# Which queue issues the transfers that turn the attention probabilities: SyncE's or GpSimd's

## The chip, the core and the metric

The kernel runs on one core of one Trainium2 chip. The metric is the device time of one execution in microseconds (us). Three runs of the kernel before took 1047.63, 1047.46 and 1044.97 us; the median is 1047.46.

Engines in the rows: PE is TensorE (PEld its weight loads), DVE is VectorE, ACT is ScalarE, POOL is GpSimd, SP is SyncE. A "q" behind an engine's name (SPq) marks an instruction of its sequencer, such as the issue of a DMA.

## The reference

One layer over 256 tokens of width 2048 in float32: RMSNorm, one input projection, eight heads of forgetting attention ("fox") and eight of differential attention, an output projection with a residual, and a gated MLP with a short causal convolution. The part that matters here is the attention of one head after its projection:

```python
s_d = einsum('bhcqd,bhckd->bhcqk', dq_b, dk_h) * diff_scale
p_d = softmax(where(chunk_mask, s_d, NEG_INF), axis=-1)
a_d = p_d[:, :, 0] - lam * p_d[:, :, 1]
o_d = einsum('bhqk,bhkd->bhqd', a_d, dv_h)
...
p_f = softmax(where(frame_mask, s_f, NEG_INF), axis=-1)
o_f = einsum('bhqk,bhkd->bhqd', p_f, fv_h)
```

The product with the values contracts over the keys, so the 256x256 probabilities of a head (stored as 128 rows of 384, since the masked quarter is left out) must be turned before TensorE can use them.

## The kernel before

Heads are numbered 1 to 16: 1 to 8 are differential, 9 to 16 are fox. The kernel goes through them in frames. Frame f has eight steps (b = 0 to 7). In each, TensorE multiplies one piece of weights for the projection of the head after f (12 matmuls of 384 columns a step: three products of operands that are split into a high and a low part; ScalarE writes the high part w_hi, L681, VectorE the low part w_lo, L1117), and between the pieces it does the attention of head f and what is left of head f-1. Every engine's program is written out in its own order, and semaphores tie them together. Nothing reorders the work at run time.

For heads 4 to 14 the probabilities are turned in two parts. VectorE transposes 32x32 blocks within its partitions (L1244, `turn_p`, writes `pdT`). Then the blocks must change places between partitions. That is done through memory: `store_p` writes `pdT` to the DRAM tensor `p_scratch` in one DMA of 192 KB (L314), and `read_p` reads it back as `p_read` in four DMAs of 48 KB each (L324), 32 partitions by 4 by 96 numbers. The chain of one head is: L1244 ends (semaphore p_turned), store issued, store landed (p_stored), four reads issued, last read landed (p_landed).

What comes after the last read differs:

- Heads 4 to 8: ScalarE copies `p_read` to `pT` (L754, `copy_p`) at step 0 of the next frame, and TensorE multiplies it with the values at step 2 of that frame (L446 to L448, `values`). After those, still at step 2, TensorE turns the q and k of the next head (L410, `transposes`), which waits for `rope_done`.
- Heads 9 to 14: TensorE reads `p_read` itself at step 5 of the next frame (L457, L458, `block_values`).

SyncE issues all DMAs: the weight pieces (L305, 384 KB each, `raw<-in_win`) and the store and the reads. Its program is one order: in frames 4 to 9 the store stands behind the load of step 3 and the reads behind that of step 5; in frames 10 to 14 both stand behind the load of step 6. A wait of the store or the reads therefore holds up the weight loads behind it, and the weight loads already in the queue stand ahead of the store's and the reads' data.

GpSimd does the rotary part for heads 1 to 8 (`rotate`: a product, L1673, and a sum, L1676), each after VectorE has normalised that head (`normed`), and two small fox tables at the end. It issues no DMA.

In the kernel after, the lines of these functions have other numbers: `store_p` is L1660, `read_p` L1670, `rotate` L1650 and L1653.

Of the kernel before, what the change touches and what calls it, by code (L numbers as in the profile page):

```python
# [9 lines left out]
ALU = mybir.AluOpType  # L10
# [3 lines left out]
P = 128  # L14
S, D, F = 256, 2048, 5504
H = 8
HD = 128
# [37 lines left out]
C_TRIG, C_ID, C_DM, C_FM, C_END = np.cumsum([0, 8 * ROPE_HALF, P, SROW, SROW]).tolist()  # L55
C_EARLY = C_DM + P
R_DG, R_BF, R_LAM, R_FG, R_END = np.cumsum([0, 8 * 2 * ROPE_HALF // 2, M * H, 4 * DQK, 2 * HD]).tolist()
# [14 lines left out]
P0, P_STOP = 4, HEADS - 1  # L72
# [9 lines left out]
def hybrid_layer_kernel(nc, xT_d, xtok_d, w0_d, win_d, wrest_d, const_d, row_d, vec_d, out_d):  # L82
    c_d = nc.dram_tensor("c_scratch", (H, S), F32, kind="Internal").ap()
    p_d = nc.dram_tensor("p_scratch", (P, SROW), F32, kind="Internal").ap()
    with ExitStack() as ctx:
# [3 lines left out]
        def sem(name):  # L89
            return ctx.enter_context(nc.semaphore(name))  # L90
# [17 lines left out]
        with ExitStack() as att:  # L108
            def sa(name, cols, dt=F32, parts=P):
                return sb(name, cols, dt, parts, att)  # L110
# [4 lines left out]
            const = sa("const", C_END)  # L115
            row = sa("row", R_END)
# [30 lines left out]
            pd, pdT, p_read = [sa(n, SROW) for n in ("pd", "pdT", "p_read")]  # L147
# [22 lines left out]
        chunk_ready, fox_landed, fox_ready = sem("chunk_ready"), sem("fox_landed"), sem("fox_ready")  # L170
# [14 lines left out]
        p_turned, p_stored, p_landed, p_copied = sem("p_turned"), sem("p_stored"), sem("p_landed"), sem("p_copied")  # L185
# [3 lines left out]
        pt_done, pT_ready, pv_done = sem("pt_done"), sem("pT_ready"), sem("pv_done")  # L189
# [25 lines left out]
        def bounced(f):  # L215

            return f - (P0 - 1)
# [54 lines left out]
        def _(sp):  # L272
# [29 lines left out]
            def load_piece(g):  # L302
                sp.wait_ge(split_done, g - RING + 1)
                if g < IN_PIECES:
                    sp.dma_start(slot(raw, g % RING, W1), win_d[(g - 8) * P:(g - 7) * P, :]).then_inc(raw_landed[g % RING], 16)  # L305
                else:
                    sp.dma_start(slot(raw, g % RING), wrest_d[(g - IN_PIECES) * P:(g - IN_PIECES + 1) * P, :]
                                 ).then_inc(raw_landed[g % RING], 16)

            def store_p(f):  # L310
                sp.wait_ge(p_turned, bounced(f))
                if f > P0:
                    sp.wait_ge(p_landed, 64 * bounced(f - 1))
                sp.dma_start(p_d, pdT[:]).then_inc(p_stored, 16)  # L314

            def read_p(f):
                sp.wait_ge(p_stored, 16 * bounced(f))
                if P0 < f <= H + 1:
                    sp.wait_ge(p_copied, bounced(f - 1))
                if f > H + 1:  # L320
                    sp.wait_ge(pv_done, f - 1)
                for j in range(4):
                    src = p_d[:, j * 3 * 32:(j + 1) * 3 * 32].rearrange("(i r) c -> r i c", i=4)
                    sp.dma_start(p_read[32 * j:32 * (j + 1), :].rearrange("r (i c) -> r i c", i=4), src).then_inc(p_landed, 16)  # L324

            def load_x_again(c):
                m, k = divmod(c, 2)
                if c == 0:
                    sp.wait_ge(xs_ready, KT)
                sp.dma_start(xT[:, c * PW:(c + 1) * PW], xtok_d[m][:, k * PW:(k + 1) * PW]).then_inc(x_again, 16)  # L330
# [5 lines left out]
            for f in range(P0, HEADS):  # L336
                for b in range(8):
                    load_piece(8 * (f + 1) + b)
                    if H + 2 <= f < H + 6 and b == 1:
                        load_x_again(f - (H + 2))  # L340
                    if f <= H + 1 and b == 3:
                        store_p(f)
                    if f <= H + 1 and b == 5:
                        read_p(f)
                    if H + 1 < f < P_STOP and b == 6:
                        store_p(f)
                        read_p(f)
                    if f == 5 and b == 6:
                        sp.wait_ge(c_ready, 1)
                        sp.dma_start(c_d, cT[:]).then_inc(c_stored, 16)  # L350
                        sp.dma_start(row[:, R_FG:R_END], row_d[0:1, R_FG:R_END].partition_broadcast(P)).then_inc(fox_landed, 16)
                        sp.dma_start(const[:, C_FM:C_FM + P], const_d[:, C_EARLY:C_EARLY + P]).then_inc(fox_landed, 16)
                    if f == 6 and b == 6:
                        sp.wait_ge(c_stored, 16)
                        sp.dma_start(cbc[:], c_d.rearrange("h s -> (h s)").partition_broadcast(P)).then_inc(cbc_landed, 16)
                        sp.dma_start(cq[:], c_d.rearrange("h (m p) -> p (h m)", p=P), allow_slow_non_contiguous=True
                                     ).then_inc(cq_landed, 16)
# [1296 lines left out]
        @block.gpsimd  # L1654
        def _(pool):

            def gain_tables():
                for m in range(M):
                    at = m * TW // M
                    table = trig[:, at:at + TW // M].rearrange("p (n a d) -> p n a d", n=4, a=2)  # L1660
                    angles = const[:, C_TRIG + m * 4 * ROPE_HALF:C_TRIG + (m + 1) * 4 * ROPE_HALF]
                    angles = angles.rearrange("p (a d) -> p a d", a=2).unsqueeze(1).to_broadcast([P, 4, 2, 2 * ROPE_HALF])
                    gains = row[:, R_DG:R_BF].rearrange("p (n d) -> p n d", n=4)
                    last = pool.tensor_tensor(table, angles, gains.unsqueeze(2).to_broadcast([P, 4, 2, 2 * ROPE_HALF]),
                                              ALU.mult)
                last.then_inc(trig_ready, 1)

            def rotate(f, p):
                pool.wait_ge(normed, f)
                q4 = qn[:, p * 2 * M * HD:(p + 1) * 2 * M * HD].rearrange("p (n d) -> p n d", d=DQK)[:, :, 0:2 * ROPE_HALF]  # L1670
                prod = rope[:, p * TW:(p + 1) * TW].rearrange("p (n a d) -> p n a d", n=8, a=2)
                table = trig[:].rearrange("p (n a d) -> p n a d", n=8, a=2)
                pool.tensor_tensor(prod, q4.unsqueeze(2).to_broadcast([P, 8, 2, 2 * ROPE_HALF]), table,  # L1673
                                   ALU.mult).then_inc(rope_prod, 1)
                pool.wait_ge(rope_prod, f)
                pool.tensor_tensor(q4.rearrange("p n (a d) -> p n a d", a=2), prod[:, :, :, 0:ROPE_HALF],  # L1676
                                   prod[:, :, :, ROPE_HALF:2 * ROPE_HALF], ALU.add).then_inc(rope_done, 1)

            pool.memset(const[:, C_DM + P:C_DM + 2 * P], 0.0)
            pool.memset(const[:, C_FM + P:C_FM + 2 * P], 0.0)  # L1680
            pool.wait_ge(const_landed, 16)
            pool.tensor_copy(const[:, C_DM + 2 * P:C_DM + 3 * P], const[:, C_DM:C_DM + P]).then_inc(chunk_ready, 1)
            pool.wait_ge(gains_ready, 1)
            gain_tables()
            pool.wait_ge(trig_ready, 1)
            with pool.Fori(0, H // 2) as i:
                rotate(i * 2 + 1, 0)
                rotate(i * 2 + 2, 1)
            pool.wait_ge(fox_landed, 32)
            pool.tensor_copy(const[:, C_FM + 2 * P:C_FM + 3 * P], const[:, C_FM:C_FM + P])  # L1690
            pool.tensor_scalar(row[:, R_FG + HD:R_FG + 2 * HD], row[:, R_FG + HD:R_FG + 2 * HD], float(HD) ** 0.5, None,
                               ALU.mult).then_inc(fox_ready, 1)


def lay_out(x, norm1_g, w_in, b_forget, fox_q_g, fox_k_g, diff_q_g, diff_k_g, lam_q1, lam_k1, lam_q2, lam_k2,
# [69 lines left out]
```

## Time and profile before

| | |
|---|---|
| median of three runs | 1047.46 us |
| the profiled execution | 1047.41 us |
| its span, first to last instruction | 1045.6 us |
| around the span | 1.8 us |
| PE busy | 1039.4 us, 99% |
| ACT busy | 785.5 us, 75% |
| DVE busy | 745.7 us, 71% |
| POOL busy | 20.5 us, 2% |
| granted TensorE clock | 1.000, in all slices |
| DMA | 217.77 MB, mean 208 GB/s |

The busy share of PE is an upper bound on how well it works, because its matmuls overlap. Here 128x384 matmuls start about every 0.163 us, the 384 columns at 2.4 GHz, and that pitch is broken in few places. The frames 4 to 15 lie between 80 and 287 us of the span.

### The profile page before, as it was taken

How to read it: one execution, taken by the hardware profiler on the slowest of the kernel's cores; microseconds unless marked ns; L12 is line 12 of the kernel's file. 1: busy time of each engine (PE TensorE's matmuls, PEld its weight loads, DVE VectorE, ACT ScalarE, POOL GpSimd, SP SyncE). 2: the span in 40 equal slices, each digit the busy share in tenths (PEclk: the TensorE clock that was granted, in tenths of full speed). 3: DMA queues.
4: the chain of work that ended last, by engine and by line, in shares of the span. 5: the costliest groups of instructions: out<-in, count | busy, mean ns of one | idle time of the engine just before them, and what ended most of it. 6: DMA issues, size and time to landing. Idle time of an engine off the chain costs nothing.

```text
span 1045.6 us, 16399 instructions
## 1 busy us (share of the span) xinstructions
PE 1039.4 (99%) x5330; PEld 941.8 (90%) x5330; DVE 745.7 (71%) x1238; ACT 785.5 (75%) x1376; POOL 20.5 (2%) x27
## 2 busy tenths in 40 slices
PE   9999999999999999999999999999999999999998
PEld 8999999999988888888888888888889988888887
DVE  6888878778767666576776776876867678866664
ACT  7777666788858884879788788798797778755553
POOL 0101010000000000000000000000000000000000
PEclk9999999999999999999999999999999999999999
DMA  9756676676766666666565575665756766666664
GB/s 355 234 160 189 193 235 201 215 245 225 237 213 198 203 199 203 202 218 201 184 221 198 187 222 194 201 216 185 219 184 187 235 204 202 203 202 206 205 206 144
DMA packets 75438, 217.77 MB, mean 208 GB/s; under 512 B 15850, under 2 KB 18418, under 8 KB 75250
## 3 DMA queue, kind: packets, MB, share of 16 engines
q1 hardware_dynamic: 75376, 216.99, 65.3%
q8 instruction: 35, 0.57, 0.2%
q14 instruction: 27, 0.20, 0.1%
HBM read 212.69 MB, written 4.27 MB: 207 GB/s over the span
## 4 chain that ended last, share of the span: by engine, by line
PE 83%; DVE 6%; DMA 4%; ACT 4%; issue 2%; SPq 1%; DVEq 0%; ACTq 0%
PE ps L605 14%; PE ps L604 14%; PE ps L606 14%; PE ps L635 7%; PE ps L633 7%; PE ps L634 7%; PE ps L397 3%; PE ps L399 3%; PE ps L398 3%; DMA raw<-in_win 3%; PE ps L582 2%; PE ps L581 2%; PE ps L580 2%; DVE w_lo L1117 2%; ACT w_hi L681 1%
## 5 line engine op out<-in xcount | busy, mean ns | idle before, releaser
L1117 DVE TENSOR_TENSOR w_lo<-raw,w_hi 128x1024 fp32r<-128x1024 f32 (+1 forms) x406 | 463.4, 1147 | 245.1 <-ACT w_hi L681 241.7
L681 ACT ACTIVATE w_hi<-raw 128x1024 fp32r<-128x1024 f32 (+1 forms) x406 | 398.1, 987 | 167.3 <-PE ps L635 74.8
L604 PE MATMUL ps<-w_hi,xs 128*128 128x512 f32 (+1 forms) x704 | 263.4, 374 | 0.0
L605 PE MATMUL ps<-w_lo,xs 128*128 128x512 f32 (+1 forms) x704 | 263.4, 374 | 0.0
L606 PE MATMUL ps<-w_hi,xs 128*128 128x512 f32 (+1 forms) x704 | 263.4, 374 | 0.0
L397 PE MATMUL ps<-w_hi,xs 128*128 128x384 f32 (+1 forms) x512 | 170.9, 334 | 0.6 <-DVE w_lo L1399 0.6
L398 PE MATMUL ps<-w_lo,xs 128*128 128x384 f32 (+1 forms) x512 | 167.0, 326 | 0.0
L399 PE MATMUL ps<-w_hi,xs 128*128 128x384 f32 (+1 forms) x512 | 167.0, 326 | 0.0
L606 PEld LDWEIGHTS ps<-w_hi,xs 128*128 128x128 f32 x704 | 133.1, 189 | 17.2
L605 PEld LDWEIGHTS ps<-w_lo,xs 128*128 128x128 f32 x704 | 133.1, 189 | 17.2
L604 PEld LDWEIGHTS ps<-w_hi,xs 128*128 128x128 f32 x704 | 133.1, 189 | 17.2
L634 PE MATMUL ps<-w_lo,a_s 128*128 128x512 f32 (+1 forms) x346 | 130.7, 378 | 0.0
L635 PE MATMUL ps<-w_hi,a_s 128*128 128x512 f32 (+1 forms) x346 | 130.7, 378 | 0.0
L633 PE MATMUL ps<-w_hi,a_s 128*128 128x512 f32 (+1 forms) x346 | 130.7, 378 | 0.0
L1005 ACT ACTIVATE uT<-utT 32x512 f32<-32x512 f32 (+1 forms) x176 | 109.4, 622 | 26.8 <-DVE utT L1529 22.8
L397 PEld LDWEIGHTS ps<-w_hi,xs 128*128 128x128 f32 x512 | 96.8, 189 | 3.4 <-issue 2.0
L398 PEld LDWEIGHTS ps<-w_lo,xs 128*128 128x128 f32 x512 | 96.8, 189 | 0.2
L399 PEld LDWEIGHTS ps<-w_hi,xs 128*128 128x128 f32 x512 | 96.8, 189 | 0.0
L633 PEld LDWEIGHTS ps<-w_hi,a_s 128*128 128x128 f32 x346 | 65.4, 189 | 9.2
L634 PEld LDWEIGHTS ps<-w_lo,a_s 128*128 128x128 f32 x346 | 65.4, 189 | 9.2
L635 PEld LDWEIGHTS ps<-w_hi,a_s 128*128 128x128 f32 x346 | 65.4, 189 | 9.2
L580 PE MATMUL ps<-w_hi,mixed 128*128 128x512 f32 x128 | 49.0, 383 | 0.0
(162 smaller groups left out, 922.1 us busy)
## 6 DMA issues: line engine op xcount, KB each, us to landing
raw<-in_wrest SPq DMA_DIRECT2D x278, 512.0 KB, 4.1
raw<-in_win SPq DMA_DIRECT2D x117, 384.0 KB, 3.8
raw<-in_wrest SPq DMA_DIRECT2D x16, 384.0 KB, 3.0
p_scratch<-pdT SPq DMA_DIRECT2D x11, 192.0 KB, 2.4
p_read<-p_scratch SPq DMA_DIRECT2D x44, 48.0 KB, 2.9
xtok<-in_xtok SPq DMA_DIRECT2D x4, 512.0 KB, 13.0
xv<-in_xtok SPq DMA_DIRECT2D x4, 512.0 KB, 6.3
raw_ahead<-in_w SPq DMA_DIRECT2D x5, 392.0 KB, 8.4
```

The source lines that it names most:

```text
L397: pe.matmul(o, xh, wh, start=(kt == 0), stop=False, skip_group_check=True)
L398: pe.matmul(o, xh, wl, start=False, stop=False, skip_group_check=True)
L399: last = pe.matmul(o, xl, wh, start=False, stop=(kt == KT - 1), skip_group_check=True)
L604: pe.matmul(o, xh, wh, start=(k == 0), stop=False, skip_group_check=True)
L605: pe.matmul(o, xh, wl, start=False, stop=False, skip_group_check=True)
L606: last = pe.matmul(o, xl, wh, start=False, stop=(k == KT - 1), skip_group_check=True)
L633: pe.matmul(to, ah, wh, start=start, stop=False, skip_group_check=True)
L634: pe.matmul(to, ah, wl, start=False, stop=False, skip_group_check=True)
L635: return pe.matmul(to, al, wh, start=False, stop=stop, skip_group_check=True)
L681: act.activation(slot(w_hi, s, w), slot(raw, s, w), ACT.Copy).then_inc(hi_ready, 1)
L1005: act.activation(dst, src, ACT.Copy).then_inc(u_moved, 1)
L1117: dve.tensor_tensor(slot(w_lo, s, w), slot(raw, s, w), f32(slot(w_hi, s, w)), ALU.subtract).then_inc(split_done, 1)
```

## The change

The store and the four reads leave SyncE's program and stand in GpSimd's. Their waits and their shapes stay as they were. GpSimd's loop over pairs of heads is written out: four rotations, then for each head from 4 to 14 the store, the four reads and, up to head 7, the rotation of the next head. The two fox tables move from the end to behind the rotation of head 7.

```diff
@@ sync
-            def store_p(f):
-                sp.wait_ge(p_turned, bounced(f))
-                if f > P0:
-                    sp.wait_ge(p_landed, 64 * bounced(f - 1))
-                sp.dma_start(p_d, pdT[:]).then_inc(p_stored, 16)
...
-                    if f <= H + 1 and b == 3:
-                        store_p(f)
-                    if f <= H + 1 and b == 5:
-                        read_p(f)
-                    if H + 1 < f < P_STOP and b == 6:
-                        store_p(f)
-                        read_p(f)
@@ gpsimd
+            def store_p(f):
+                pool.wait_ge(p_turned, bounced(f))
+                if f > P0:
+                    pool.wait_ge(p_landed, 64 * bounced(f - 1))
+                pool.dma_start(p_d, pdT[:]).then_inc(p_stored, 16)
+
+            def read_p(f):
+                pool.wait_ge(p_stored, 16 * bounced(f))
+                if P0 < f <= H + 1:
+                    pool.wait_ge(p_copied, bounced(f - 1))
+                if f > H + 1:
+                    pool.wait_ge(pv_done, f - 1)
+                for j in range(4):
+                    src = p_d[:, j * 3 * 32:(j + 1) * 3 * 32].rearrange("(i r) c -> r i c", i=4)
+                    pool.dma_start(p_read[32 * j:32 * (j + 1), :].rearrange("r (i c) -> r i c", i=4), src).then_inc(p_landed, 16)
...
-            with pool.Fori(0, H // 2) as i:
-                rotate(i * 2 + 1, 0)
-                rotate(i * 2 + 2, 1)
-            pool.wait_ge(fox_landed, 32)
...
+            for f in range(1, P0 + 1):
+                rotate(f, 1 - f % 2)
+            for f in range(P0, P_STOP):
+                store_p(f)
+                read_p(f)
+                if f < H:
+                    rotate(f + 1, f % 2)
+                if f == 6:
+                    pool.wait_ge(fox_landed, 32)
...
```

On SyncE, in frames 4 and 5 before, the weight loads (L305) and the store (L314) and reads (L324) of heads 4 and 5 alternate:

```order
L305 DMA raw<-in_win 128x768 [waits split_done] x4
L314 DMA p_scratch<-pdT 128x384 [waits p_turned]
L305 DMA raw<-in_win 128x768 [waits split_done] x2
L324 DMA p_read<-p_scratch 32x4x96 [waits p_stored]
L324 DMA p_read<-p_scratch 32x4x96 x3
L305 DMA raw<-in_win 128x768 [waits split_done] x6
L314 DMA p_scratch<-pdT 128x384 [waits p_landed,p_turned]
L305 DMA raw<-in_win 128x768 [waits split_done] x2
L324 DMA p_read<-p_scratch 32x4x96 [waits p_copied,p_stored]
L324 DMA p_read<-p_scratch 32x4x96 x3
```

Now the same place of SyncE's program holds weight loads alone, and the first other transfer is that of the forget gates:

```order
L305 DMA raw<-in_win 128x768 [waits split_done] x15
L327 DMA c_scratch<-cT 8x256 [waits c_ready]
L328 DMA row<-in_row 128x256
L329 DMA const<-in_const 128x128
```

No weight load stands behind a wait for p_turned or p_stored any more. On GpSimd, the loop of rotations before (one pass is two heads), and the two fox tables behind it:

```order
L1673 TENSOR_TENSOR rope<-qn,trig 128x256 [waits normed]
L1676 TENSOR_TENSOR qn<-rope 128x8x16 [waits rope_prod]
L1669 REGISTER_ALU
L1673 TENSOR_TENSOR rope<-qn,trig 128x256 [waits normed]
L1676 TENSOR_TENSOR qn<-rope 128x8x16 [waits rope_prod]
L1686 REGISTER_ALU
L1686 COMPARE_AND_BRANCH
L1690 COPY const<-const 128x128 [waits fox_landed]
```

Now, on GpSimd, the rotation of head 4, the store and reads of head 4, the rotation of head 5, the store and reads of head 5, and the rotation of head 6:

```order
L1650 TENSOR_TENSOR rope<-qn,trig 128x256 [waits normed]
L1653 TENSOR_TENSOR qn<-rope 128x8x16 [waits rope_prod]
L1660 DMA p_scratch<-pdT 128x384 [waits p_turned]
L1670 DMA p_read<-p_scratch 32x4x96 [waits p_stored]
L1670 DMA p_read<-p_scratch 32x4x96 x3
L1650 TENSOR_TENSOR rope<-qn,trig 128x256 [waits normed]
L1653 TENSOR_TENSOR qn<-rope 128x8x16 [waits rope_prod]
L1660 DMA p_scratch<-pdT 128x384 [waits p_landed,p_turned]
L1670 DMA p_read<-p_scratch 32x4x96 [waits p_copied,p_stored]
L1670 DMA p_read<-p_scratch 32x4x96 x3
L1650 TENSOR_TENSOR rope<-qn,trig 128x256 [waits normed]
L1653 TENSOR_TENSOR qn<-rope 128x8x16 [waits rope_prod]
```

A rotation now stands behind the store and the reads of the head before it.

## Rows read from the trace of the kernel before

**Rows 1.** Page, part 1: busy time of PE (share of the span) and instructions.
```profile
PE 1039.4 (99%) x5330; PEld 941.8 (90%) x5330; DVE 745.7 (71%) x1238; ACT 785.5 (75%) x1376; POOL 20.5 (2%) x27
```

**Rows 2.** Waits of PE, whole span: waited for, us in total, times, longest.
```profile
PE ps L513 <- DVE warm_r L1411: 1.4, 1, 1.4
PE ps L446 <- ACT pT L754: 1.0, 2, 0.6
```

**Rows 3.** Waits of SP's queue, 85 to 290 us.
```profile
SPq L314 <- DVE pdT L1244: 17.8, 11, 2.5
SPq L324 <- DMA p_scratch<-pdT: 12.3, 5, 2.7
```

**Rows 4.** Timeline, DVE: the turns of heads 4 to 8 (start, duration).
```profile
91.58 0.58 DVE L1244 STREAM_TRANSPOSE pdT<-pd 128x384 f32<-128x384 f32 x1
110.49 0.58 DVE L1244 STREAM_TRANSPOSE pdT<-pd 128x384 f32<-128x384 f32 x1
128.51 0.58 DVE L1244 STREAM_TRANSPOSE pdT<-pd 128x384 f32<-128x384 f32 x1
147.72 0.58 DVE L1244 STREAM_TRANSPOSE pdT<-pd 128x384 f32<-128x384 f32 x1
165.25 0.58 DVE L1244 STREAM_TRANSPOSE pdT<-pd 128x384 f32<-128x384 f32 x1
```

**Rows 5.** Timeline, PE: first value product of heads 4 to 8 [idle before].
```profile
100.62 0.38 PE L446 MATMUL ps<-qkv,pT 128*128 128x128 f32 x2
119.47 0.49 PE L446 MATMUL ps<-qkv,pT 128*128 128x128 f32 x2 [0.56 <-ACT pT L754]
137.55 0.38 PE L446 MATMUL ps<-qkv,pT 128*128 128x128 f32 x2
156.21 0.38 PE L446 MATMUL ps<-qkv,pT 128*128 128x128 f32 x1 [0.48 <-ACT pT L754]
174.29 0.27 PE L446 MATMUL ps<-qkv,pT 128*128 128x128 f32 x1
```

**Rows 6.** Timeline, ACT: the copies of heads 5 and 7.
```profile
118.89 0.52 ACT L754 ACTIVATE pT<-p_read 128x384 f32<-128x384 f32 x1 [2.09 <-DMA p_read<-p_scratch]
155.63 0.52 ACT L754 ACTIVATE pT<-p_read 128x384 f32<-128x384 f32 x1 [1.61 <-DMA p_read<-p_scratch]
```

**Rows 7.** Timeline: turns and value products of heads 10 and 14.
```profile
205.27 0.58 DVE L1244 STREAM_TRANSPOSE pdT<-s_sb 128x384 f32<-128x384 f32 x1
273.04 0.58 DVE L1244 STREAM_TRANSPOSE pdT<-s_sb 128x384 f32<-128x384 f32 x1
214.74 0.38 PE L457 MATMUL ps<-p_read,qkv 128*128 128x256 f32 x1
282.50 0.38 PE L457 MATMUL ps<-p_read,qkv 128*128 128x256 f32 x1
```

**Rows 8.** Tile pdT, 90 to 170 us: ns min/median/max; landing from issue start.
```profile
L314 SPq DMA_DIRECT2D p_scratch<-pdT x5: 326/326/327, 92.2 to 165.9; - x5
...
DMA to landing us min/median/max: 1.8/1.8/1.9
```

**Rows 9.** Tile p_read, 90 to 176 us (heads 4 to 8).
```profile
L324 SPq DMA_DIRECT2D p_read<-p_scratch x20: 348/432/433, 94.3 to 169.4; - x20
...
DMA to landing us min/median/max: 2.8/3.2/4.3
```

**Rows 10.** Tile p_read, 200 to 285 us (heads 10 to 14).
```profile
DMA to landing us min/median/max: 1.7/1.9/2.3
```

**Rows 11.** GpSimd's two instructions of a rotation, whole span: ns min/median/max.
```profile
L1673 POOL TENSOR_TENSOR rope<-qn,trig x8: 735/1378/1441, 40.4 to 154.0; 128x256 f32<-128x256 f32 x8
L1676 POOL TENSOR_TENSOR qn<-rope x8: 459/1048/1054, 41.2 to 155.5; 128x128 f32<-128x128 f32 x8
```

**Rows 12.** Timeline, POOL: the rotation of head 6.
```profile
116.81 1.38 POOL L1673 TENSOR_TENSOR rope<-qn,trig 128x256 f32<-128x256 f32 x1 [15.62 <-DVE qn L1173]
118.27 1.04 POOL L1676 TENSOR_TENSOR qn<-rope 128x128 f32<-128x128 f32 x1
```

More of the change, by code:

```diff
@@ L308, in load_piece @@
                                  ).then_inc(raw_landed[g % RING], 16)
-            def store_p(f):
-                sp.wait_ge(p_turned, bounced(f))
-                if f > P0:
-                    sp.wait_ge(p_landed, 64 * bounced(f - 1))
-                sp.dma_start(p_d, pdT[:]).then_inc(p_stored, 16)
[L316 to L324, printed above, removed]
             def load_x_again(c):
@@ L1685, in _ @@
             pool.wait_ge(trig_ready, 1)
-            with pool.Fori(0, H // 2) as i:
-                rotate(i * 2 + 1, 0)
-                rotate(i * 2 + 2, 1)
-            pool.wait_ge(fox_landed, 32)
-            pool.tensor_copy(const[:, C_FM + 2 * P:C_FM + 3 * P], const[:, C_FM:C_FM + P])
-            pool.tensor_scalar(row[:, R_FG + HD:R_FG + 2 * HD], row[:, R_FG + HD:R_FG + 2 * HD], float(HD) ** 0.5, None,
-                               ALU.mult).then_inc(fox_ready, 1)
+            for f in range(1, P0 + 1):
[7 more added lines that the diff above has]
+                    pool.wait_ge(fox_landed, 32)
+                    pool.tensor_copy(const[:, C_FM + 2 * P:C_FM + 3 * P], const[:, C_FM:C_FM + P])
+                    pool.tensor_scalar(row[:, R_FG + HD:R_FG + 2 * HD], row[:, R_FG + HD:R_FG + 2 * HD], float(HD) ** 0.5,
+                                       None, ALU.mult).then_inc(fox_ready, 1)
 def lay_out(x, norm1_g, w_in, b_forget, fox_q_g, fox_k_g, diff_q_g, diff_k_g, lam_q1, lam_k1, lam_q2, lam_k2,
```

## The prediction

> **What bounds the kernel now.** I read the page's busy times first, then PE's waits, then the timeline of one head after another. TensorE is busy for 1039.4 of 1045.6 us [rows 1], and its longest waits are 1.4 us at the start and 1.0 us, in two pieces, for the copy of the turned probabilities, `pT` [rows 2]. Those two are all that this change could give back on TensorE. SyncE's queue, which the change relieves, waited 17.8 us for p_turned and 12.3 us for p_stored [rows 3]. The reader is to see that these 30 us are no loss: a weight load that leaves late costs something only when TensorE waits for its piece, and no such wait stands among those of PE. What can cost time is the other end, the round trip of the probabilities, which has little room.
>
> **The room of the round trip.** For each head I measure from the end of the turn (L1244) to the moment at which TensorE would start the value product if the data were there. At heads 4 to 8 the copy stands between: it starts at 155.63 and the product, which waited for it, at 156.21 [rows 5, 6], so 0.60 us lies between landing and product. The last read may land this long after the turn's end without a wait:
>
> - head 4: 100.62 - 0.60 - 92.16 = 7.86 us
> - head 5: 119.47 - 0.56 (the wait) - 0.60 - 111.07 = 7.24
> - head 6: 137.55 - 0.60 - 129.09 = 7.86
> - head 7: 156.21 - 0.48 - 0.60 - 148.30 = 6.83
> - head 8: 174.29 - 0.60 - 165.83 = 7.86 [rows 4, 5]
>
> Their sum is 37.65 us. At heads 10 to 14 TensorE reads `p_read` itself, and I allow 0.1 us behind the landing: 214.74 - 0.1 - 205.85 = 8.79 for the first, 282.50 - 0.1 - 273.62 = 8.78 for the last of the five [rows 7]. Head 9 has a frame of room more and never counts.
>
> **The round trip, part by part.** It is a store, whose data must land, and then four issues one behind the other, of which the last must land. Call one issue c and the landing of the last read behind its issue's end r. The landing of the store behind its issue's end was 1.8 - 0.33 = 1.5 us [rows 8]. With 0.03 us of hand-over twice, the trip is L = 0.06 + c + 1.5 + 4c + r = 1.56 + 5c + r.
>
> - c on SyncE is 0.33 us for the store and 0.43 for a read [rows 8, 9]. GpSimd issues no DMA in this trace, so its price has to be bounded. The low end is SyncE's 0.43 us, if issuing is all sequencer work. The high end is the longer of GpSimd's own instructions, 1.38 us [rows 11]. I take 1.05 us, the median of its shorter one (L1676), since each issue has to make up the addresses of 128 rows on GpSimd itself, which is work of that size.
> - r was long while the reads stood behind two weight loads in SyncE's queue: 2.8 to 4.3 us from the issue's start, the longest for the last of four [rows 9]. For the last read this is about 3.3 us behind the issue's end (my reading of the five heads: 3.9 at most, 4.3 - 0.43). Without loads ahead it is 1.9 - 0.43 = 1.5 [rows 10]. In a queue of its own the read no longer stands behind the loads, but still shares the DMA engines with them. I take the middle, 2.4 us.
>
> So L = 1.56 + 5.25 + 2.4 = 9.2 us. Before, it was 118.87 - 111.07 = 7.8 us at head 5 (the copy began at 118.89 [rows 6]).
>
> **The sum.** At heads 4 to 8 TensorE would be late by 5 x 9.2 - 37.65 = 8.35 us in all, of which 1.04 us is already there (0.56 + 0.48), so 7.3 us are new. At heads 10 to 14 it is 5 x (9.2 - 8.8) = 2.0 us. Nothing catches this up: TensorE has no gap elsewhere, and the turn of the next head follows TensorE's scores, which shift along. Together 9.3 us, on the profiled execution's 1047.4 us: 1056.7 us. Its time agrees with the median (1047.46), so the ratio stands for both.
>
> What else moves, and what I cost at nothing:
>
> - The rotation of head f+1 stands behind the reads of head f on GpSimd. For head 6 it started at 116.81 [rows 12]. GpSimd would be free 0.06 + 5 x 1.05 + 1.5 = 6.8 us after the turn, at 117.9. The rotation (1.38 + 1.04 us and a hand-over) would end at 120.4. TensorE's transposes wait for it, but they stand behind the value product, which would start at 111.07 + 9.2 + 0.6 = 120.9. It hides by 0.5 us behind the very wait that I price; if the landing is quick and the issues slow, it comes out instead, within the same tenths.
> - ScalarE waits in `copy_p` with its splits behind it. It waited 2.09 and 1.61 us at heads 5 and 7 [rows 6] and TensorE never missed a piece. Now the wait is some 1.4 us longer, but TensorE stands too, at step 2 of the same frame, with the pieces of the next steps already split.
> - The written-out program drops a few branches of GpSimd, and the fox tables come earlier, far ahead of their use in frame 8. Nothing.
> - The weight loads leave earlier. That is 30 us of SyncE's waits [rows 3] which bought no wait of TensorE, so nothing, except that more of them are under way during the reads, which is in r.
>
> Each 0.1 us of c is 0.5 us per head and 5 us on ten heads. The price is therefore known badly, and the direction better than the size.
>
> **What the skill says.** The Trainium skill (SBUF — State Buffer, "Who interferes with whom") says that VectorE's two-port modes shut GpSimd out of the write side with which it writes DMA descriptors, while a VectorE operation on two SBUF inputs competes only with GpSimd's reads. Rows 11 show GpSimd's own two instructions at 735 and 459 ns at best and 1378 and 1048 in the median; by the page it is reads that suffer, and the issues, which only write, would stay below these medians.
>
> **Rivals.**
>
> - *Cheap issue.* GpSimd's issues cost what SyncE's do, and its own queue spares the reads the two loads ahead. Then c = 0.43, r = 1.5 and L = 5.2 us, below all ten allowances: both waits of 1.04 us go and nothing comes, so 1046.4 us. It decides from L below about 7.6, which with r = 2.4 is c below 0.72 us. For it speaks that transfers of SyncE without loads ahead land in 1.9 us. Against it speaks that no POOL instruction on this much data in the middle of the kernel took under 1 us [rows 11]. The same skill (DMA: Bandwidth & Descriptors, "Anatomy of one DMA — SWDGE (gpsimd) path") gives 2.0 us plus bytes over 436 GB/s for a whole DMA from GpSimd and calls descriptor generation small. By the page a store would be 2.45 us and a read 2.1, an estimate of L near 6 us and 1046.4 us; no run here shows it.
> - *Issues beside VectorE's work.* Each issue is stretched as GpSimd's product is, to c = 1.38 us. With r = 2.4 L is 10.9 us, so heads 4 to 8 lose 54.5 - 37.65 - 1.04 = 15.8 us and heads 10 to 14 lose 5 x 2.1 = 10.5: 1074 us. For it: VectorE is at work 71% of the span [rows 1]. Against it: an issue need not read SBUF.
> - *Reads slow as before.* c = 1.05 but r = 3.3, because the weight loads that are now never held back fill the DMA engines: L = 10.1, and heads 4 to 8 lose 11.8, heads 10 to 14 6.5: 1065.7 us. It is the upper part of my own case.
>
> **Chances.** Forecast with its neighbours (c from 0.9 to 1.25, r from 1.5 to 3.3): 0.53. Cheap issue: 0.27. Stretched issues, or a first DMA of GpSimd that costs extra: 0.20. The predicted time is that of the likeliest, 1057 us; its own range is 1050 to 1066. The range for 8 in 10 runs from 1045.5 (cheap issue, with the scatter of the three runs) to 1073 us. A measurement of this kernel can tell about 0.3%, 3.1 us, from no change. Faster by over that would need more than the 1.04 us that can be given back: 0.03. Within it falls the cheap issue and a little of the forecast's lower edge: 0.25. Slower: 0.72.
>
> **What would show it.** In the profile after: PE's wait on `pT` (L446) at all of heads 4 to 8, 8.4 us in five pieces, and a new one at L457 for the reads of heads 10 to 14, 2 us in five. From the end of the turn to ScalarE's copy 9.2 us instead of 7.8 at head 5, with POOL's five issues about 1.05 us apart. SyncE's waits for p_turned and p_stored gone without a gain. It is wrong if the issues stand under 0.7 us apart and PE's wait at L446 goes to zero, or if PE begins to wait for w_lo, which would make the weight path the cause.

## The result, and the profile after

The changed kernel took 1056.33 us (median of six runs, 1054.89 to 1057.72) against 1047.05 for the kernel before (six runs): a ratio of 1.0093, 95% interval 1.0083 to 1.0104. The forecast was 1056.7. The number was right, but that it came so close is luck: of the forecast's two costs one was right in place and near in size (7.3 us forecast, 6.0 found), the other hardly appeared (2.0 forecast, 0.1 found), and a third that was not foreseen, 3.4 us of half clock, took their room.

The profiled execution of the changed kernel has a span of 1055.1 us, 9.5 more than before. In its page, part 1 and part 3 (queue, kind: packets, MB, share of the DMA engines):

```profile
PE 1043.7 (99%) x5330; PEld 946.3 (90%) x5330; DVE 745.7 (71%) x1238; ACT 785.8 (74%) x1376; POOL 50.7 (5%) x82
...
q1 hardware_dynamic: 67456, 212.66, 61.2%
q0 software_dynamic: 2112, 4.33, 1.5%
```

The probabilities go through a queue of their own kind now, and GpSimd is busy with issuing. PE's busy time rose by 4.3 us with the same 5330 instructions, which a wait cannot do; a slower clock can. The waits of PE, to be set against [rows 2]:

```profile
PE ps L423 <- ACT pT L731: 7.0, 3, 3.8
PE ps L490 <- DVE warm_r L1388: 1.5, 1, 1.5
```

L423 is the value product (L446 before). It waits 7.0 us instead of 1.0, in three pieces. The turns of heads 4 to 8, the copies and the value products on the timeline, which answer to [rows 4 to 6]:

```profile
91.30 0.58 DVE L1221 STREAM_TRANSPOSE pdT<-pd 128x384 f32<-128x384 f32 x1
110.79 0.58 DVE L1221 STREAM_TRANSPOSE pdT<-pd 128x384 f32<-128x384 f32 x1
132.65 0.58 DVE L1221 STREAM_TRANSPOSE pdT<-pd 128x384 f32<-128x384 f32 x1
156.33 0.58 DVE L1221 STREAM_TRANSPOSE pdT<-pd 128x384 f32<-128x384 f32 x1
174.47 0.58 DVE L1221 STREAM_TRANSPOSE pdT<-pd 128x384 f32<-128x384 f32 x1
...
100.42 0.52 ACT L731 ACTIVATE pT<-p_read 128x384 f32<-128x384 f32 x1 [2.03 <-DMA p_read<-p_scratch]
121.49 0.52 ACT L731 ACTIVATE pT<-p_read 128x384 f32<-128x384 f32 x1 [4.21 <-DMA p_read<-p_scratch]
145.17 0.52 ACT L731 ACTIVATE pT<-p_read 128x384 f32<-128x384 f32 x1 [5.28 <-DMA p_read<-p_scratch]
164.78 0.53 ACT L731 ACTIVATE pT<-p_read 128x384 f32<-128x384 f32 x1 [1.21 <-DMA p_read<-p_scratch]
183.01 0.52 ACT L731 ACTIVATE pT<-p_read 128x384 f32<-128x384 f32 x1 [1.57 <-DMA p_read<-p_scratch]
...
101.00 0.38 PE L423 MATMUL ps<-qkv,pT 128*128 128x128 f32 x1 [0.50 <-ACT pT L731]
122.06 0.38 PE L423 MATMUL ps<-qkv,pT 128*128 128x128 f32 x1 [2.70 <-ACT pT L731]
145.75 0.38 PE L423 MATMUL ps<-qkv,pT 128*128 128x128 f32 x1 [3.76 <-ACT pT L731]
```

From the end of the turn to the copy it is now 8.5, 10.1, 11.9, 7.9 and 8.0 us, 9.3 in the mean. The forecast had 9.2 for each. The mean is right and the spread is the story: heads 5 and 6 carry 6.5 of the 7.0 us. Two rows of the chain of waits show head 6 (start, us, what): the first three issues of its reads, and the last read from the start of its issue to its landing:

```profile
136.10 1.63 POOL p_read L1670 x3
137.72 7.42 DMA p_read<-p_scratch
```

The last read took 7.4 us to land. What ran beside it is on SyncE's timeline, the 1 MB load of the forget gates for all heads, `cbc`, here in the kernel after:

```profile
136.96 0.33 SPq L332 DMA_DIRECT2D cbc<-c_scratch  x1
```

In the kernel before, it stood behind these reads in the same queue:

```profile
131.25 1.80 SPq L324 DMA_DIRECT2D p_read<-p_scratch  x4
133.10 0.43 SPq L305 DMA_DIRECT2D raw<-in_win  x1
133.57 0.43 SPq L355 DMA_DIRECT2D cbc<-c_scratch  x1
```

There the last read, issued at 132.6 us and so 0.9 us ahead of `cbc`, landed after 3.4 us. Now `cbc` falls amid the four reads: issued at 136.1, 136.6, 137.2 and 137.7, they took 4.0, 5.8, 6.6 and 7.4 us. Only the first, as far ahead of `cbc` as the last one was before, is as quick as at other heads.

On GpSimd a read's issue takes 0.55 us, not 1.05, and the store's 0.59. Its groups by line (busy us, mean ns, idle before), and the landing of the reads of heads 4 to 8 from the start of their issue, against [rows 9, 11]:

```profile
L1670 POOL DMA_DIRECT2D p_read<-p_scratch x44 | 23.9, 550 | 23.0 <-DMA p_scratch<-pdT 23.0
...
L1660 POOL DMA_DIRECT2D p_scratch<-pdT x11 | 6.5, 594 | 136.4 <-DVE pdT L1221 136.4
```
```profile
DMA to landing us min/median/max: 2.8/3.8/7.4
```

Behind each of the two long waits the clock that TensorE was granted fell, 0.8 and 1.0 us after the wait's end. Two stretches of 6 us from the changed kernel (columns as named in the first line), then 122 to 128 us of the kernel before:

```profile
core 0: us, PE busy (x) PEld busy (x) DVE busy (x) ACT busy (x) POOL busy (x), PEclk, DMA share, GB/s
122.00:128.00 6.00, 5.94 (x31) 5.38 (x32) 3.08 (x8) 3.99 (x12) 0.00 (x0) 0.72 0.46 149
146.00:152.00 6.00, 6.00 (x33) 5.44 (x33) 3.32 (x11) 3.68 (x11) 0.00 (x0) 0.72 0.75 257
```
```profile
122.00:128.00 6.00, 6.00 (x41) 5.42 (x41) 4.08 (x21) 3.98 (x14) 0.00 (x0) 1.00 0.61 189
```

A mean of 0.72 over 6 us is 0.28 x 6 = 1.7 us of full clock lost, twice: 3.4 us. Within such a stretch, 3.4 us long, the level is 1.2 GHz instead of 2.4. The chain shows it as a pitch of 0.32 us instead of 0.16:

```profile
147.32 0.32 PE ps L374
147.64 0.32 PE ps L375
```

New waits, 7.0 - 1.0 = 6.0 us, and 3.4 us of clock make 9.4 of the 9.5 us. The sum closes better than it should. Two short waits outside this chain, 0.6 us for w_lo at 8.7 us and 0.3 us for `pT` at 293.7 us, are in the kernel before and not in this one, and PE's busy time rose by 0.9 us more than the clock explains; these two about cancel, and where the 0.9 us come from was not found. Nor is the clock's share the same in each execution: in two of the six (1054.89 and 1055.36 us) the mean granted clock was 0.998 and not 0.996 or 0.997, which is one such stretch and not two.

### The profile page after: what moved, and what is told of

The parts are those of the page before. It is cut to its first block, busy times and chain, and to the rows that moved or that the text cites. A ratio compares the mean times of both kernels' runs of the same rounds, so it can differ in the third digit from the quotient of the medians.

```text
span 1055.1 us, 16381 instructions
## 1 busy us (share of the span) xinstructions
PE 1043.7 (99%) x5330; PEld 946.3 (90%) x5330; DVE 745.7 (71%) x1238; ACT 785.8 (74%) x1376; POOL 50.7 (5%) x82
## 4 chain that ended last, share of the span: by engine, by line
PE 95%; issue 2%; DMA 2%; POOL 0%; DVE 0%; ACT 0%; POOLq 0%; DVEq 0%
PE ps L581 14%; PE ps L582 14%; PE ps L583 14%; PE ps L612 7%; PE ps L610 7%; PE ps L611 7%; PE ps L374 7%; PE ps L375 7%; PE ps L376 7%; PE ps L557 3%; PE ps L559 3%; PE ps L558 3%; DMA p_read<-p_scratch 1%; PE ps L396 1%; PE ps L490 0%
## 5 line engine op out<-in xcount | busy, mean ns | idle before, releaser
L1094 DVE TENSOR_TENSOR w_lo<-raw,w_hi 128x1024 fp32r<-128x1024 f32 (+1 forms) x406 | 463.1, 1146 | 249.3 <-ACT w_hi L658 246.3
```

The source lines that it names most:

```text
L1094: dve.tensor_tensor(slot(w_lo, s, w), slot(raw, s, w), f32(slot(w_hi, s, w)), ALU.subtract).then_inc(split_done, 1)
```

## The experiments

All ratios are against the kernel before, run on the same chip in turns. The first four kernels ask whether the forget-gate transfers and the clock make the loss.

**All forget-gate transfers later** (in the changed kernel; the first pair of lines moves c_scratch, row and const, the second cbc and cq):

```diff
-                    if f == 5 and b == 6:
+                    if f == 6 and b == 1:
-                    if f == 6 and b == 6:
+                    if f == 7 and b == 1:
```

> The changed kernel, with the forget-gate transfers (c_scratch, row, const) moved from step 6 of frame 5 to step 1 of frame 6, and cbc and cq from step 6 of frame 6 to step 1 of frame 7, so that they no longer run beside the reads of heads 5 and 6. Theory A (the loss is two late round trips, because these transfers share the DMA engines with the reads, and TensorE's half clock behind each long wait): the last read of heads 5 and 6 lands about 4 us after its issue as at heads 4, 7 and 8, PE's wait for pT falls from 7.0 to 1 to 2 us, no half clock, about 1048.5 us. Theory B (GpSimd's slower issue and hand-over make the loss at every head): the waits stay, 1055 us or more.

1050.77 us (1049.59 to 1055.38), ratio 1.0041 [1.0025, 1.0057]: more than half of the loss is gone, not all of it. The profiled execution was the slowest of its runs (1055.38) and shows why not. Head 6's trip fell to 8.2 us, but `cbc`, issued at 142.7 us, now ran beside the store of head 7. Its landing, alone in this window:

```profile
L1660 POOL DMA_DIRECT2D p_scratch<-pdT x1: 618/618/618, 150.6 to 150.6; - x1
...
DMA to landing us min/median/max: 5.8/5.8/5.8
```

It is 2.3 us in the changed kernel. PE then waited 3.4 us at head 7, and a half-clock stretch of 3.4 us came with it. The mean clock of the other four runs was 1.00, so without that stretch. The large transfer hurts whatever part of a round trip it meets.

**Only cbc and cq later:**

```diff
-                    if f == 6 and b == 6:
+                    if f == 7 and b == 1:
```

> The changed kernel with only cbc and cq moved to frame 7, step 1; the small transfers of frame 5 stay. Theory A: the wait at head 6 (3.8 us) and its half-clock stretch (about 1.6 us) go, those at head 5 (3.0 us and about 1.6) stay: 1051.5 us. Theory B: 1055 us or more. If head 5's wait also goes, the small transfers were not its cause.

1050.84 us (1049.60 to 1054.33), ratio 1.0049 [1.0030, 1.0068]. The same as with all of them moved, so no cost of the small transfers is to be seen. In this execution head 5's wait was 1.6 us and not 3.0, though they stayed:

```profile
PE ps L423 <- ACT pT L731: 3.6, 5, 1.6
```

The clock stayed at 1.00. In two of the six runs, the slowest ones (1053.85 and 1054.33 us), it was 0.998. Why head 5 waited 2.7 us in the changed kernel is therefore not settled: its trip was 9.0 to 10.2 us in the four kernels that read on GpSimd's queue with the small transfers in place, and 9.5 and 8.7 us in the two without.

**Fillers in the two long waits** (changed kernel):

```diff
                     if trail and b == TRAIL_AT["values"]:
+                        if f in (6, 7):
+                            pe.wait_ge(rowmax_done, f - 1)
+                            for _ in range(12 if f == 6 else 16):
+                                pe.matmul(scratch, warm_r[:, 0:P], weave(warm_r[:]), start=True, stop=True,
+                                          skip_group_check=True)
                         values(f - 1, par, "diff")
```

> The changed kernel with 12 and 16 filler matmuls of 512 columns on TensorE (2.6 and 3.4 us) in front of the value products of heads 5 and 6; their result is not used. Theory A with the clock as a term of its own: the waits' time stays lost but the granted clock stays at 1.00, which gives back about 3.3 us: 1053 us. Rival (the half clock costs nothing that the waits would not cost anyway): no change against the changed kernel, 1056 us; if the fillers overrun the waits, more.

1055.63 us (1054.82 to 1056.08), ratio 1.0084 [1.0065, 1.0103]. The granted clock was 1.00 throughout, as expected, but only 0.7 us came back. In the profiled execution the other value products waited 2.0 us more than in the changed kernel's (2.6 us against 0.6, at heads 4, 7, 8, 10 and 14), and heads 5 and 6 came 0.2 and 0.7 us later. That is 2.9 us, which eats most of the 3.4. Since round trips scatter by about 1 us from one execution to the next, this kernel could not tell the clock's cost from that scatter. The pair of made waits below was built for it.

**All of them later, in the kernel before:** the same edit as in the first.

> The kernel before with the same five transfers moved as in the first kernel. Theory A: SyncE issued the reads ahead of them in the same queue, so little changes: within 1 us of 1047. Rival (these transfers cost the kernel before too): ACT's wait for p_read at head 5 (2.09 us) shortens and PE's 0.56 us at head 5 goes, at most 1 us faster.

1047.49 us, ratio 1.0010 [1.0000, 1.0019]. In the old queue order these transfers cost nothing that moving them would give back.

The next four ask which half of the change costs, and whether it is GpSimd.

**cbc by head** (changed kernel, row and const at step 1 of frame 6 too):

```diff
-                        sp.dma_start(cbc[:], c_d.rearrange("h s -> (h s)").partition_broadcast(P)).then_inc(cbc_landed, 16)
...
+                    if 7 <= f < HEADS - 1 and b == 1:
+                        sp.dma_start(tile(cbc, f - 7), c_d[f - 7:f - 6, :].partition_broadcast(P)).then_inc(cbc_landed, 16)
...
+                dve.wait_ge(cbc_landed, f * 16 - 16 * H)
```

> The changed kernel with the small forget-gate transfers at step 1 of frame 6, and cbc (1 MB in one DMA) cut into eight DMAs of 128 KB, one per head, at step 1 of frames 7 to 14. In the kernels with the whole cbc moved to frame 7 it lengthened the store of head 7 instead (3.6 and 5.2 us to landing against 2.0). Theory A (the large transfer beside the round trip): no head has a long store or a long last read; round trips of 8 to 9 us at heads 4 to 8, PE's wait for pT 3 to 4 us in all, clock 1.00 throughout, 1049.5 us. Rival (every read of GpSimd's queue is slow, whatever runs beside): as the kernel with cbc moved, 1051 us or more.

1049.67 us, and its six runs lie within 1.2 us (1049.14 to 1050.32); ratio 1.0035 [1.0022, 1.0047]. The trips of heads 4 to 8 are 8.0 to 8.9 us, and the longest of their reads lands after 4.2 us:

```profile
DMA to landing us min/median/max: 2.9/3.7/4.2
```

So 3.3 us of the 9.3 are left where no large transfer meets a round trip: the cost of GpSimd's longer trip (in this profile PE waits 2.4 us for `pT` at heads 4 to 8, and 0.8 us for the reads of heads 10 and 14). The other 6 went with the large transfer moved and cut. Moving it whole had left 4.5 us (1050.84 against 1046.32 in the same round), so cutting it is worth about 1 us more, which is not clear of the noise. Not all of the 6 need be `cbc`'s: head 5 waited before `cbc` was issued, and its wait, 2.7 us with a half-clock stretch behind it in the changed kernel, is 1.3 us with none here.

**Only the store on GpSimd:** `read_p` back on SyncE at its old places (`f <= H + 1 and b == 5`, later frames `b == 6`).

> The changed kernel with only the store on GpSimd, the four reads back on SyncE at their old places. Theory A: the store lands about 0.7 us later after the turn than on SyncE (hand-over 0.3 us, issue 0.6 instead of 0.33, landing as before), the reads stand ahead of the forget-gate transfers again; round trips 0.7 us longer than before, PE's wait at pT 3 us instead of 1: 1049 us. Rival (the store's issue is what costs): most of the 9 us, 1053 us or more.

1046.77 us (ten runs), ratio 1.0003 [0.9993, 1.0013]: no difference to before. I had expected 2 us more. The store did land later after its turn, at head 5 at 113.03 - 110.48 = 2.6 us instead of 1.9, but SyncE, which p_turned no longer holds, issued the reads at once, 2.6 us behind the turn instead of 2.2, and these landed sooner (median 2.9 instead of 3.2):

```profile
DMA to landing us min/median/max: 2.5/2.9/4.3
```

**Only the reads on GpSimd:** `store_p` back on SyncE at its old places.

> The changed kernel with only the four reads on GpSimd, the store on SyncE at its old place. Theory A: the reads' landing stays at 3.6 us in the median and 5 to 7 us for the last at heads 5 and 6, so both long waits stay, some 0.6 us shorter, and with them the half clock: 1054 us. Rival: near 1049 us.

1055.03 us (1053.20 to 1057.92), ratio 1.0084 [1.0059, 1.0110]: nearly the whole loss. PE waited 5.0 us at head 6 and the clock was at half for 6.8 us around the end of that wait; behind head 5's 1.8 us it stayed at 1.00. The last read of head 6 took 9.2 us beside `cbc`, which SyncE had issued at 134.0 us, in the middle of GpSimd's four issues:

```profile
DMA to landing us min/median/max: 3.3/4.1/9.2
```

**Reads from ScalarE's queue** (kernel before, reads of heads 4 to 9 behind ScalarE's split of step 5):

```diff
                     if trail and b == 0 and f > P0:
                         copy_p(f - 1)
+                    if trail and b == 5:
+                        read_p(f)
```

> The kernel before with the reads of heads 4 to 9 issued by ScalarE behind its split of step 5 (the hardware queue of ScalarE, store and heads 10 to 14 on SyncE). Tells the kind of queue from the sharing of the DMA engines. If sharing with the weight loads and the forget-gate transfers is what lengthens the last read, it lands 3 to 4 us behind its issue, and 5 us or more at heads 5 and 6 once more: 1050 to 1053 us. If it is GpSimd's software queue, a read lands 2 us behind its issue at all heads, PE never waits for pT: 1046.3 us, unless ScalarE's 1.7 us of issues a head delay its splits, which would show as PE waiting for w_lo.

1058.10 us, ratio 1.0122 [1.0105, 1.0139], slower than I had expected, and for another reason. ScalarE stands in `read_p` until the store has landed (4.08 us at head 5, the idle time before L772), so its evacuations, the next head's norm and its rotation come late:

```profile
116.80 0.47 ACT L772 ACTIVATE mixed<-ps,sg 128x256 fp32r<-128x256 f32 x1 [4.08 <-issue]
```
```profile
PE ps L408 <- POOL qn L1686: 4.7, 4, 1.2
PE ps L444 <- ACT pT L752: 2.7, 5, 0.9
PE ps L395 <- DVE w_lo L1127: 1.6, 1, 1.6
```

Its landings answer the question put to it in part: a queue of hardware, with no weight loads ahead in it, and the reads still need 3.3 to 4.3 us beside the loads of the other queue.

```profile
DMA to landing us min/median/max: 3.3/3.6/4.3
```

This comparison suggests, though one kernel does not show it, that the ordinary length of the reads in GpSimd's queue (3.7 to 3.8 in the median) comes from sharing the DMA engines and not from its kind of queue. Whether a hardware queue would suffer from `cbc` as GpSimd's does stays open: here SyncE issued it at 139.5 us, when the reads of head 6 were through.

The next two price the clock, in the kernel before. TensorE waits for seven memsets of GpSimd in front of the value products of heads 5 and 6, once empty (`range(0)`), once with 15 fillers.

```diff
+                        if f in (6, 7):
+                            pe.wait_ge(rowmax_done, f - 1)
+                            for _ in range(15):
+                                pe.matmul(scratch, warm_r[:, 0:P], weave(warm_r[:]), start=True, stop=True,
+                                          skip_group_check=True)
+                            pe.wait_ge(dly, 7 * (f - 5))
...
+                if f in (7, 8):
+                    pool.wait_ge(piece_used, 8 * (f - 1) + 3)
+                    for k in range(7):
+                        if k or f == 8:
+                            pool.wait_ge(dly, 7 * (f - 7) + k)
+                        pool.memset(dly_t[:], 0.0).then_inc(dly, 1)
```

> The kernel before, with TensorE made to wait in front of the value products of heads 5 and 6 for seven memsets of GpSimd (128x512 each, one behind the other, begun when step 2's piece is multiplied; estimated 4 us). Nothing else is moved. Theory A (half clock behind a long wait is a cost of its own): two waits of W us each, read from the trace, and behind each a stretch of matmuls at a 0.32 us pitch instead of 0.16, 1.6 us more each: before + 2W + 3.3 us, near 1058 us for W = 4. Rival (the waits alone): before + 2W.

> The same, with 15 filler matmuls of 512 columns (3.2 us) on TensorE in each of the two waits; their result is not used. Theory A: the same waits, no half clock, 3.3 us less than the kernel with the empty waits. Rival: the same time.

Empty: 1058.85 us (1058.45 to 1059.81), ratio 1.0118 [1.0102, 1.0133]. Filled: 1055.40 (1054.74 to 1055.69), ratio 1.0085 [1.0069, 1.0100]. So a half clock is a cost of its own: the difference is 3.45 us for two waits, where 3.3 was expected. The empty waits are 4.47 and 4.49 us. The waits are alike, but the stretches are not; here is the second wait, and then the clock behind the first and behind the second:

```profile
147.31 0.55 PE L447 MATMUL ps<-qkv,pT 128*128 128x128 f32 x1 [4.49 <-issue]
```
```profile
123.00:130.00 7.00, 6.84 (x38) 6.31 (x39) 2.34 (x13) 2.52 (x9) 0.06 (x1) 0.78 0.17 62
147.00:154.00 7.00, 6.69 (x28) 6.30 (x30) 1.25 (x6) 1.69 (x9) 0.21 (x1) 0.54 0.56 200
```

The half level held for 3.4 us at the first and 6.8 us at the second, and began 0.4 and 0.7 us before the wait ended. By the profile that is 1.5 and 3.1 us lost, 4.6 together, in an execution that was 4.45 us slower than the filled kernel's. The medians give 3.45, single runs 2.8 to 5.1. So the expected 1.6 us each was met at one wait only, and that 3.45 lies so near 3.3 is chance. With fillers 1.2 us of each wait is left and the clock is 1.00:

```profile
121.00:128.00 7.00, 5.81 (x38) 4.74 (x37) 2.13 (x8) 2.51 (x9) 2.37 (x5) 1.00 0.51 165
```

The last two look for a version that beats both.

**Reads one step earlier** (kernel before, `f <= H + 1 and b == 4`):

> The kernel before, with the reads of heads 4 to 9 behind the load of step 4 instead of step 5. One weight load instead of two stands ahead of them: the last read lands some 1 us earlier, PE's wait for pT (1.04 us before) goes: 1 us faster at most, 0.1%, unless the load of step 5, now behind p_stored, is late; then PE waits for w_lo.

1047.10 us, ratio 1.0006 [0.9997, 1.0015]. The reads landed in 2.3 us in the median instead of 3.2, and PE's wait for pT went, but 0.6 us for the rotation (L410) and 0.3 for the turned q and k (L419) came in its place:

```profile
DMA to landing us min/median/max: 1.9/2.3/4.0
```
```profile
PE ps L410 <- POOL qn L1676: 0.6, 1, 0.6
```

**Store on GpSimd and reads one step earlier:**

> Store on GpSimd, reads on SyncE behind the load of step 4. The store's wait for the turn no longer holds up SyncE, the reads have one load ahead. If both small terms hold, no wait for pT and at most 1 us under the kernel before; if not, the same as it.

1047.89 us, ratio 1.0019 [1.0009, 1.0028]: a little slower, with new waits of the same kind (1.1 us for the turned q and k, 0.5 for the rotation). No version beat the kernel before.

## Why the prediction was right, and where it was not

- *TensorE is the bound, and 1.04 us is all there is to gain.* Held. SyncE's waits for p_turned and p_stored are gone from the profile after, and no kernel here came out clearly under the one before. The store alone, which frees SyncE of its wait for the turn, gave 1.0003.
- *The room of the round trip.* Held as a mechanism, and it is what made the forecast possible; the sizes were off. Read in the same way from the profile after, the rooms of heads 4 to 8 are 8.0, 7.4, 8.2, 8.0 and 7.9 us, 39.5 in all instead of 37.65. The trips sum to 46.4, and 46.4 - 39.5 = 6.9 is what PE waited. By the forecast's rooms heads 7 and 8 would have waited 1.0 and 0.1 us; they did not. Head 7's room was 8.0 us too in the kernel before with the forget-gate transfers moved, which suggests that its 6.83 had to do with their place; that was not tested alone, nor why the others grew.
- *c, the issue on GpSimd, 1.05 us.* Too high: 0.59 for the store and 0.55 for a read. On the other hand GpSimd's issue begins 0.3 us behind its release and not 0.03 (turn's end at 111.37, store at 111.67 at head 5), once for the store and once for the reads. The four reads are issued one right behind the other. So 1.56 + 5.25 = 6.8 us up to the last issue's end was really 5.0 to 5.7.
- *r, the landing of the last read, 2.4 us behind its issue.* Too low: 2.7 to 2.9 us at heads 4, 7 and 8, 5.1 and 6.9 at heads 5 and 6, and 3.5 to 4.2 at heads 10 to 14. I had taken that a queue of its own spares the reads a part of the wait for the weight loads. It spares little: at heads 4, 7 and 8 the same term was 2.8 to 3.7 us before. At heads 10 to 14 it costs, 1.4 to 1.9 us before: there SyncE, standing in its waits, issued no load from 204.9 to 210.8 us around head 10, and now it issues three between 217.9 and 221.2, beside the reads. The errors in c and r cancelled in the mean of L (9.3 against 9.2 at heads 4 to 8, 9.1 at heads 10 to 14), which is luck and not a confirmation of either.
- *7.3 us new at heads 4 to 8.* Measured 6.0, in three pieces, not five; the difference is the larger room. What I did not see in the diff is an order that it takes away: before, the reads of head 6 were issued ahead of `cbc` in one queue, and I counted the loads ahead of the reads but not the transfers kept behind them. The runs show it: by the medians it loses 4.5 us with `cbc` moved and 3.3 with `cbc` moved and cut by head, not 9.3.
- *2.0 us at heads 10 to 14.* Hardly there: PE shows no wait for these reads in the list above. Their trips were 8.7 to 9.2 us, as forecast, but the room was also larger than the 8.5 to 8.8 of before: 224.39 - 0.1 - 215.25 = 9.0 at head 10 and 9.1 to 9.2 at the others. Why the turn comes sooner there, relative to TensorE, was not tested.
- *Nothing for the clock.* Wrong. 3.4 us by the profile. The made waits show that it is a cost of its own (3.45 us for two by the medians), though not that it is 1.7 us a wait: their stretches cost 1.5 and 3.1. It stands where the missing 1.3 and 1.9 us of the two terms above should be, so the sum came out at 9.5. That is luck too.
- *The rotation behind the reads, ScalarE's splits, the written-out program: nothing.* Held. PE waits neither for the rotation nor for w_lo in the profile after; the rotation of head 6 began at 117.29, 0.9 us behind the last issue.
- *The rivals.* Cheap issue was right about c (0.55) and wrong about r, and so about the time. The issues stand under 0.7 us apart, which was half of my own sign of being wrong; the other half, PE's wait going to zero, did not come. Issues stretched by VectorE's work are refuted: all 44 issues of the reads took 0.548 to 0.565 us, and the seven that lay wholly beside a two-input operation of VectorE (L1094) 0.548 to 0.553, those that met none of these 0.548 to 0.563. Here the trace agrees with the Trainium skill (SBUF — State Buffer, "Who interferes with whom"), which infers that writing descriptors is not held up by VectorE's two-input operations. The Trainium skill's other rule (DMA: Bandwidth & Descriptors, "Anatomy of one DMA — SWDGE (gpsimd) path") fits the store, 2.3 us in the median where it gives 2.45, and calls the issue small, which 0.55 us nearly is; for a read it gives 2.1 us and the median here is 3.8, beside the weight loads, so the measurement decides. Reads slow as before was the nearest description of the landings.

## What to carry to other kernels

Moving transfers to another queue removes waits behind them and also the order between them: list which transfers stood behind the moved ones in the old queue, because those now run beside them, and one of 1 MB can make a 48 KB read twice as long. If the bounding engine is busy all the time, measure how much later the moved chain may end before it waits, and compare that room with the new chain; a freed issuing queue is worth nothing without a wait of the bounding engine behind it. A wait of TensorE in full stream may cost more than its length, since the matmuls behind it can run at half clock: here waits of 2.7 us and more cost 1.5 to 3.1 us on top, and waits of up to 2.1 us nothing. Fill it or count it. And check a forecast by its terms: this one hit the total to 0.4 us with most of its terms off.

## What the runs showed of the hardware

- Issue on GpSimd's queue: 0.55 us for 48 KB in 128 rows of 384 bytes, 0.59 us in the mean for 192 KB in 128 rows (0.74 for the first), back to back, and 0.3 us from release to start. On SyncE 0.43, 0.33 and 0.03.
- A 48 KB read beside 384 KB weight loads lands, in the median, 3.2 us after its issue starts in SyncE's queue behind two loads, 3.6 in ScalarE's and 3.8 in GpSimd's; with one load ahead in SyncE's queue 2.3, with none ahead and none issued meanwhile 1.9. Beside the 1 MB transfer the last one took 7.4 and 9.2 us in GpSimd's queue.
- With waits of TensorE of 2.70, 3.38, 3.76 and 4.47 us the granted clock was at half for 3.4 us, and with waits of 4.49 and 5.03 us for 6.8 us. The stretches began between 2.4 us before and 1.0 us behind the end of the wait, and slowed the matmuls behind it by 1.7, 1.7, 1.7, 1.5, 3.1 and 2.2 us. With the waits of up to 2.1 us in the profiled executions the clock stayed at 1.00.
